# A finer step grid for two attention blocks that run inside an expert-lookup loop

## What is computed

```
def stick_breaking_mixer(xn, k_sh, v_sh, w_q, w_out):      # 8 heads of 128, 4 query blocks of 128 tokens
    q = (xn @ w_q) ... / sqrt(128)
    for i in range(nq):                                     # block i sees key blocks 0..i
        z = einsum('bhqd,bhnsd->bhqns', qi, kb)
        log_keep = where(mask, log_sigmoid(-z), 0.0)
        cs_in = einsum('bhqnj,js->bhqns', log_keep, tri)    # suffix sums inside a block
        after = cumsum of the block sums, from the right
        a = where(mask, exp(z + cs_in + after), 0.0)
        outs.append(einsum('bhqns,bhnsd->bhqd', a, vb))
    return o @ w_out

def peer_ffn(xn, w_q, subkeys, u, v):
    ...                                                     # top-16 products of two key sets -> experts, gates
    hid = einsum('cd,ced->ce', xc, take(u, ec))
    w = gates * gelu(hid)
    return einsum('ce,ced->cd', w, take(v, ec))
```

## Time and profile before

| | us |
|---|---|
| median of 3 runs | 2712.43 (2710.35 to 2717.75) |
| the profiled execution, its own time | 2710.35 |
| its span in the trace | 2708.4 |
| TensorE matmul busy | 2095.0 (77%) |
| VectorE busy | 1676.4 (62%) |
| ScalarE busy | 778.5 (29%) |
| wave 2 and 3 (side 0), us 918.8 to 1306.9 | 388.1 |
| wave 4 and 5 (side 1), us 1306.9 to 1761.7 | 454.8 |
| wave 1 and wave 6 for comparison (no side) | 160.9 and 161.1 |

### The profile page before, as it was taken

The page is one execution under the profiler, slowest core; times in us unless marked ns, Lnnn a source line. Parts: engine busy times, 40 slices in busy tenths (PEclk is TensorE's granted clock), DMA queues, the critical chain, the costliest instruction groups (busy, mean ns, idle before and its releaser), DMA issues. The chain is left out here.

```text
span 2708.4 us, 29262 instructions
## 1 busy us (share of the span) xinstructions
PE 2095.0 (77%) x10702; PEld 1138.3 (42%) x10702; DVE 1676.4 (62%) x3916; ACT 778.5 (29%) x1702; POOL 599.7 (22%) x585
## 2 busy tenths in 40 slices
PE   2999776957776698889698878865665799956786
PEld 2445476343231165454265445311110544435564
DVE  5988875258978676544768645498644247444542
ACT  1100232024233423532434542233323111141221
POOL 0111000023444333433333323343431000000000
PEclk9999866978897799999799888877776899976889
DMA  7788500049999999999899888999996121100000
GB/s 303 286 326 316 206 1 1 31 183 421 412 420 421 419 417 410 421 403 387 331 394 363 311 295 336 393 421 421 415 421 269 53 78 62 62 11 1 9 8 16
DMA packets 103696, 707.77 MB, mean 261 GB/s; under 512 B 11232, under 2 KB 14176, under 8 KB 26368
## 3 DMA queue, kind: packets, MB, share of 16 engines
q0 software_dynamic: 83520, 608.21, 56.2%
q1 hardware_dynamic: 20032, 97.69, 9.3%
HBM read 702.45 MB, written 3.41 MB: 261 GB/s over the span
## 5 line engine op out<-in xcount | busy, mean ns | idle before, releaser
L1309 PE MATMUL ps<-got,diag 64*64 64x512 f32 x4096 | 681.5, 759 | 348.1 <-ACT diag L1380 326.4
L1415 DVE CUSTOM_DVE_ANT_0 got<-got,xk 128x1024 f32<-128x1024 f32 x512 | 616.9, 1223 | 274.3 <-DMA got<-in_peer_uv,idx 269.5
L1330 POOL DMA_INDIRECT got<-in_peer_uv,idx x512 | 563.2, 1100 | 942.2 <-PE ps L1309 844.0
L1309 PEld LDWEIGHTS ps<-got,diag 64*64 64x64 f32 x4096 | 132.0, 154 | 736.4 <-ACT diag L1380 642.4
L1375 ACT ACTIVATE gelu<-eye,hid 128x64 f32<-128x64 f32 x512 | 176.6, 345 | 678.3 <-DVE hid L1415 673.6
L253 PE MATMUL ps<-xT,ring 128*128 128x512 f32 x704 | 307.3, 594 | 2.3 <-PEq L353 1.2
L292 DVE SCALAR_TENSOR_TENSOR hgrn_in_psums<-vring,vec,hgrn_in_psums 128x256 f32<-128x256 f32 x420 | 203.7, 485 | 15.0
L253 PEld LDWEIGHTS ps<-xT,ring 128*128 128x128 f32 x704 | 132.6, 190 | 161.9 <-issue 161.0
L1380 ACT ACTIVATE diag<-gelu,gate 128x64 f32<-128x64 f32 x512 | 178.0, 348 | 48.9 <-ACT gelu L1375 1.1
L827 PE MATMUL ps<-xT,ring 128*128 128x256 f32 x768 | 190.1, 397 | 0.3 <-ACT xT L940 0.3
L253 PE MATMUL ps<-ring,xT 128*128 128x512 f32 (+1 forms) x448 | 182.0, 563 | 5.2 <-PEq L1513 3.7
(11 more groups left out here) (477 smaller groups left out, 2374.3 us busy)
## 6 DMA issues: line engine op xcount, KB each, us to landing
vring<-in_vslabs POOLq DMA_DIRECT2D x68, 1024.0 KB, 5.2
ring<-in_slabs SPq DMA_DIRECT2D x22, 2048.0 KB, 9.0
ring<-in_small SPq DMA_DIRECT2D x80, 512.0 KB
got<-in_peer_uv,idx POOLq DMA_INDIRECT x512
h<-in_x SPq DMA_DIRECT2D x1, 2048.0 KB, 15.8
out<-h SPq DMA_DIRECT2D x4, 512.0 KB, 3.0
bias_rows<-rows SPq DMA_DIRECT2D x1, 1280.0 KB, 5.2
keys<-in_keysT SPq DMA_DIRECT2D x2, 512.0 KB
```

The source lines that it names most:

```text
L1309: mm = nc.tensor.matmul(ps[to:to + HALF, i, :], diag[own, n % NDIAG, :], got[own, n % GRING, 1, 512 * g:512 * g + 512], start=(k == 0), st ...
L1330: nc.gpsimd.indirect_dma_start(out=got[:, n % GRING].rearrange("p a d -> p (a d)"), out_offset=None, in_=table, in_offset=bass.IndirectOff ...
L1415: nc.vector.tensor_tensor_reduce(row_in, row_in, xk[:, w % 2, :], 1.0, 0.0, ALU.mult, ALU.add, hid[:, w % 2, k:k + 1]).then_inc(dotted, 1)
```

## The change

The numbers of the plan are changed, and two things in the code. The query projection of a head, one step with 8 matmuls before, is now two half jobs of 4 matmuls in two steps, as the other jobs have it. Results are taken out earlier: turns 1 step after the job instead of 2, key and ask jobs 2 steps after their first half instead of 4, value and back jobs 3. The gaps between the phases shrink by a step each. The heads of side 0 go by a pitch of 7 steps instead of 6, with `total` one step earlier and `expo`, `output` one later; in side 1 the pitch stays 6, with `return` one step earlier. The cost function that paces the steps gets 0.9 for each step and loses its floor of 6.0 for a step with `soft`. Side 0 has 125 steps instead of 127, side 1 has 142 instead of 148, spread over the same 107 slots each. No instruction is added or removed on TensorE; a line is added ahead of the loop lines, so L1309 of before is L1310 after.

```diff
-        each, pitch = (1 if p else 2), 6
-        asks = [(0, -4, -2)] if p else [(0, -7, -5), (1, -4, -2)]
-        stages = {"product": 0, "take": 2, "soft": 2, "top": 4, "sums": 4, "total": 7, "expo": 8, "output": 9, "return": 11}
+        each = 1 if p else 2
+        pitch, asks = (6, [(0, -5, -4, -3)]) if p else (7, [(0, -8, -6, -5), (1, -5, -2, -1)])
+        stages = {"product": 0, "take": 2, "soft": 2, "top": 4, "sums": 4, "total": 7 if p else 6, "expo": 8 if p else 9,
+                  "output": 9 if p else 10, "return": 10 if p else 11}
...
             if kind == "turn":
                 job_at.setdefault(s, []).append((n, kind, i, 1))
-                evac_at.setdefault(s + 2, []).append((n, kind, i))
+                evac_at.setdefault(s + 1, []).append((n, kind, i))
             else:
...
-                evac_at.setdefault(s + 4, []).append((n, kind, i))
+                evac_at.setdefault(s + (3 if kind in ("value", "back") else 2), []).append((n, kind, i))
...
-            c = sum(0.45 if job[1] == "turn" else 1.8 for job in plan["job_at"].get(s, []))
-            c += 3.6 if s in plan["query_at"] else 0
+            c = 0.9 + sum(0.45 if job[1] == "turn" else 1.8 for job in plan["job_at"].get(s, []))
+            c += 1.8 if s in plan["query_at"] else 0
...
-            c = max(c, 6.0 if (s, "soft") in plan["stage_at"] else 0.6)
...
-                    a = plan["query_at"][s]
+                    a, half = plan["query_at"][s]
...
-                    for half in range(2):
-                        mm = by_columns(query_bank, w, half)
-                    mm.then_inc(job_done, 1)
+                    mm = by_columns(query_bank, w, half)
+                    if half:
+                        mm.then_inc(job_done, 1)
```

More of the change, by code:

```diff
@@ L702, in side_plan @@
         jobs += [(s + j // 2, "turn", j) for j in range(4)]
-        s += 4
+        s += 3
         jobs += [(s + 2 * i, "key", i) for i in range(H)]
@@ L708, in side_plan @@
         jobs += [(s + j // 2, "turn", 4 + j) for j in range(4)]
-        head = s + 4 - min(q[1] for q in asks)
+        head = s + 3 - min(q[1] for q in asks)
         s = head + pitch * (H // each - 1) + stages["return"] + 1
         jobs += [(s + 2 * i, "back", i) for i in range(H)]
-        s += 2 * H + 3
+        s += 2 * H + 2
         at |= {"squares2": s, "mean2": s + 2, "root2": s + 2, "scale2": s + 3}
@@ L715, in side_plan @@
         jobs += [(s + j // 2, "turn", 8 + j) for j in range(4)]
-        s += 4
+        s += 3
         jobs += [(s + 2 * i, "ask", i) for i in range(H)]
-        steps = s + 2 * H + 3
+        steps = s + 2 * H + 1
         job_at, evac_at, query_at, query_out_at, stage_at = {}, {}, {}, {}, {}
@@ L726, in side_plan @@
                     job_at.setdefault(s + half, []).append((n, kind, i, half))
-                evac_at.setdefault(s + 4, []).append((n, kind, i))
+                evac_at.setdefault(s + (3 if kind in ("value", "back") else 2), []).append((n, kind, i))
         for g in range(H // each):
-            for i, made_, out_ in asks:
-                query_at[head + pitch * g + made_] = each * g + i
+            for i, first, second, out_ in asks:
+                query_at[head + pitch * g + first] = (each * g + i, 0)
+                query_at[head + pitch * g + second] = (each * g + i, 1)
                 query_out_at[head + pitch * g + out_] = each * g + i
@@ L860, in pe_side @@
                 if s in plan["query_at"]:
-                    a = plan["query_at"][s]
+                    a, half = plan["query_at"][s]
                     w = small_slab("query", a)
-                    if a == 0:
+                    if half == 0 and a == 0:
                         pe.wait_ge(turn_act, 8)
@@ L866, in pe_side @@
                         pe.wait_ge(*bank_free)
-                    else:
+                    elif half == 0:
                         pe.wait_ge(query_out, a)
-                    for half in range(2):
-                        mm = by_columns(query_bank, w, half)
-                    mm.then_inc(job_done, 1)
+                    mm = by_columns(query_bank, w, half)
+                    if half:
+                        mm.then_inc(job_done, 1)
                 if (s, "product") in plan["stage_at"]:
```

## The result

The changed kernel takes 2740.41 us (median of six runs, 2730.76 to 2742.39), the kernel before beside it 2712.47 (2708.25 to 2717.75): a ratio of 1.0095, interval [1.0076, 1.0114]. It is slower, as forecast, but by 28 us and not by 9; 2740 lies outside the range. The profiled executions took 2742.39 (span 2739.9) and 2710.35. Of the 31.5 us between the two spans 28.3 lie in the waves with sides and 4.3 ahead of the expert loop, where the kernels do not differ and its start scatters between 591.6 and 600.8 us in the profiles of this document.

A forecast was written before the change was run, and what follows sets the result against it. TensorE was taken to be bound by its work plus waits for ScalarE's late diagonals, with DMA a close second bound in side 0. Gap and clock terms summed to +8.9 us: 2719.3 profiled, 2721 in medians, range over the cases 2704 to 2734.

The forecast's parts named there:

- the three gaps: Side 0, behind the first three soft slots: TensorE gaps of 3.6, 4.3 and 4.3 us, together +8.4.
- the turn places: Four places where turns are taken out a step earlier: gap behind 2.61 instead of 1.61, +4.0 us.
- -0.5: Side 1's terms together, among them heads -5.2, first query +0.3 and last back +1.3 us.
- rival A: Side 0's gaps absorbed by the gathers, side 1's round trip shorter in all heads: about -8, 2704 us; chance 0.17.
- the -4.3 of the first queries: Side 0, first queries: the gap of 2.58 and the slow projection behind it vanish, -4.3 us.
- the clock term: Side 0, behind the three new soft gaps: TensorE's lower clock charged twice at 1.6, +3.2 us.
- wave 3: Start of wave 3: copy cover lost +0.7, late-gather gap -2.6 and slow product -1.1 gone; together -3.0 us.
- Near 59: TensorE's idle time in waves 2 and 3, side 0, forecast near 59 us.
- The gaps at the end of the heads: Side 0, last group's total, expo, output and return in neighbouring slots: gaps 6.3 against 3.6, +2.7 us.
- C: Clock falls for longer in side 0 (5 us), gap of 0.5 in half of 32 jobs (8): 2733 us; chance 0.14.
- B: No change: half the losses absorbed, no clock penalty, +1 to +3, 2714 us; chance with D 0.27.
- D: Copy-out order does not bite on ScalarE: gaps stay 2 to 3, sum about +2; chance with B 0.27.

The follow-up runs named there:

- fallen clock: Changed kernel with 7 unused matmuls behind each of side 0's four soft steps, the diagonals no earlier: 2733.05 us, 1.0073.
- coupling and cover: Copy-out waiting directly ahead of ScalarE's block, and TensorE's work during the block; both undone in the changed kernel by whole queries in side 0: 2729.3 us, 1.0064.
- whole queries: Changed kernel, side 0's even query halves in neighbouring steps, odd query whole in the soft step, copy-outs apart from the block: 2729.3 us, 1.0064.
- turns and phases: Changed kernel with turns taken out 2 steps behind, asks 3, and the old gaps between phases, both sides: 2726.04 us, 1.0047.
- costs and whole queries: Changed kernel with the old pacing costs and whole queries in side 0: 2721.37 us, 1.0018.
- costs and clock: Changed kernel with the old pacing costs in side 0 and 7 unused matmuls behind each of its four soft steps: 2721.32 us, 1.0014.
- whole queries and turns: Changed kernel with whole queries in side 0 and the old turns, asks and phase gaps: 2716.63 us, 1.0010.
- spread plan: Changed kernel with the old pacing costs in side 0, which spread its heads' steps over more slots: 2723.59 us, 1.0022; with whole queries besides, 2721.37 us, 1.0018.
- the run with all remedies: Changed kernel with whole queries in side 0, old turns, asks and phase gaps, and old pacing costs on both sides: 2735.07 us, 1.0060.
- the nine places: Old side 0 with changed side 1 but old turns and asks (2708.7 us, 0.9981), plus 4 to 8 unused matmuls at nine idle places: 2698.98 us, 0.9939.
- the run with new costs in side 0 alone: Kernel before with its old plan, side 0's steps spread by the new pacing costs: 2721.4 us, 1.0009.

## Why the prediction was wrong

**Right: the local mechanisms and most gap lengths.** Copy-out in front of the block, the three gaps to within 0.1 us, the turn places 2.6 instead of 1.6, the last asks 1.15. In the 64 half jobs only two gaps stand, of 1.25 and 0.67 us among side 0's values (before one of 0.91). Side 1 made no measurable difference (1.0009), as -0.5 said, but that is in part luck: behind `soft` of the second, third and fourth head the gaps fell from 3.03, 3.03 and 2.43 to 1.83, 2.87 and 1.70, and the first head's, which the forecast left alone, grew from 1.84 to 4.56.

**Wrong: "TensorE's work is the same before and after, matmul by matmul; only gaps ahead of slots change. I add up their changes."** This is the step that failed. It gave the pacing costs no term in side 0, and it took every gap for time lost or won. The reason given against rival A, "busy and idle time adding up to the stretch", cannot carry that: busy and idle time of any engine add up to any stretch, whatever sets its length. Where the work lies decides whether a gap counts. The share of 1.02 in the earlier trace rows was read as a floor for gains and as no help to losses ("a longer one costs, since nothing but TensorE's queue sets it"); in fact the floor also hid TensorE's delays, as long as its work and its waits together stayed under the gathers' 2.76 us a slot. The new costs fill the slots of the heads with 2.85 us of work, and nothing is hidden any more. Undone alone they give back 14.6 of side 0's 25.3 us; put alone into the old plan they cost 4.2. The same step failed for the gains: ahead of the heads the gathers bind as well (share 1.01 and 1.02), and that stretch took 165.9 us before and 166.2 after, although it lost 21 records of work and its forecast change was the -4.3 of the first queries and one turn's +1.0. The gap of 2.58 there is gone, but that behind the turns is now directly ahead of the queries: 3.11 us (2.61 before), with 1.84 more inside the turns and the first half in 3.18 us instead of 1.99.

**Wrong: the clock term, "+3.2 (bounds 0 and 5)".** With the 2.8 that the terms for the first queries and wave 3 took off again, the forecast left TensorE's busy time of side 0 about where it was; it rose by 11.7 (of which some 3 may be scatter: the same old side 0 read 331.9 to 338.2 in three profiles). The term was for the three new gaps, and their rows have 2.6, 2.2 and 1.6, together 6.4 us: twice the forecast and above its upper bound of 5. The trace had a price, 1.67 us behind a gap of 2.58; I charged two gaps of three, at the price of a shorter one, and not the turn places, whose gaps of 2.61 stood in the earlier trace rows. The Trainium skill, TensorE: Matmul & The Clock Gate, "Why this matters for your kernels", advises against idle gaps between bursts; the trace agrees for the three soft gaps, all of which paid.

**Idle time.** "Near 59" was also a slip: 53.6 and the sum's own gap terms for side 0, 9.0, make 62.6. It came to 67.3. The gaps at the end of the heads sum to 6.5 (forecast 6.3) and the fourth soft gap is 4.8 (5.3 less 0.7), so the excess lies elsewhere: two gaps of 0.6 and 1.8 at the start of wave 3, where 0.7 was to be left, 1.8 us inside turn jobs that waited for VectorE and 0.5 more behind them, 1.0 more among the values, and less than half a microsecond at each of some other slots.

**The rivals.** A, that the gathers absorb side 0's losses, had the right question and the wrong answer: they mostly do where the steps are spread (3.9 and 3.6 us left at most), not in this plan. C, the clock, was the nearest in time (2733), and half right in mechanism: the fallen clock lasts for a slot and the step behind it, as in the earlier trace rows, but the gap of 0.5 in the 32 jobs did not come. That its time came near is luck: of its two terms, the 8 us for the 32 jobs never came. B and D fell.

**How the 25.3 us divide.** The remedies overlap, so there is no one division. Undone alone: costs 14.6, coupling and cover (whole queries) 11.4, fallen clock 8.2, turns and phases 4.3. Undone together: costs and whole queries 18.5, costs and clock 18.2, whole queries and turns 13.8, each read from one profile. About 7 us stay in every version of the new side 0. With whole queries in the spread plan side 0 is 2.4 us behind the old one at slot 204, 6.1 at slot 210 and 6.8 at its end. `total`, `expo`, `output` and `return` of the last group stand in neighbouring slots there. In the run with all remedies their gaps are 1.99, 2.33 and 1.36 us, where the kernel before has 1.99 and 1.07, so the 2.7 us that the forecast had for them are real. No run has put those steps back alone, and what else is in the 7 us stays open.

## What to carry to other kernels

A sum of gap changes holds only while the same resource sets the time; when a change also moves where work lies, first compare each stretch's work per slot with the floor of the other resource, and price the stretches in which the order of the two flips. One pacing rule need not suit two stages: spread steps where transfers bind, pack them where a long block on another engine needs cover. And a gap is to be charged with the clock behind it: in these sides always when it is over 3.6 us long, and in three cases of four from 2.6 us on.

## What the runs showed of the hardware

- **Unused work that keeps TensorE from pausing pays, even though it shortens no wait**: 0.9939 against 0.9981 for the nine places, with intervals that do not touch, and in the profile 8.2 us of side 0 for 28 matmuls (56 records).
- **The fall of the clock has no sharp bound in these traces.** I counted TensorE's gaps in the sides of all 18 profiles by whether the granted clock read 1.2 GHz anywhere in the 5 us behind them: it did behind 44 of 138 gaps of 1.5 to 2.05 us, 97 of 128 gaps of 2.55 to 3.0, and all 95 of over 3.6. The same gap went both ways. In the kernel before two slots took 1.95 us behind 3.03; with the same plan in side 1, in the run with new costs in side 0 alone, they took 3.69:

```profile
1475.39 3.69 PE L1314 MATMUL ps<-got,diag 64*64 64x512 f32 x16 [3.03 <-ACT diag L1385]
```

S1 was 454.8 and 459.9 us in these two, so a stretch of one profile carries about 5 us of such scatter, and only the timed rounds decide differences of that size.
- **TensorE's busy time is not a fixed cost.** The same old side 0 was busy for 334.5, 331.9 and 338.2 us in three profiles and took 388.1, 388.4 and 387.9: while the gathers bind, a slower clock only eats idle time.
